# A hybrid RG-LRU / GLA / PEER step on one core: weight slabs laid out on the host, 8 KB per partition and slab instead of 1 KB

## The reference

```python
for l in range(DEPTH):                       # DEPTH = 2
    mod_p = ada_mod(c_ctx[None], ada_w[l], ada_b[l])      # silu(cond) @ ada_w[l], 1024 x 6144
    mod_s = ada_mod(c, ada_w[l], ada_b[l])
    hp = pre_mod(xp, norm1_g[l], mod_p[0], mod_p[1])      # rmsnorm * (1 + scale) + shift
    ...
    # l even: proj = xm @ rg_w_in (1024 x 2048); conv; block-diagonal gates (rg_wa, rg_wi);
    #         linear scans in both directions; (gelu(gate) * h) @ rg_w_out (1024 x 1024)
    # l odd:  proj = xm @ gla_w_in (1024 x 3104: q, k, v, g and 32 columns z);
    #         chunked GLA in both directions; (silu(g) * norm(o)) @ gla_w_out (1024 x 1024)
    xp = xp + mod_p[2] * op
    xp = xp + mod_p[5] * peer(pre_mod(xp, norm2_g[l], mod_p[3], mod_p[4]), *pp)

def peer(xm, wq, k1, k2, u_tab, v_tab):      # 8 heads, 16 experts of 16384 per token and head
    q = xt @ wq                              # wq 1024 x 2048, 256 columns per head
    # scores against two sets of 128 keys, top 16 of each, top 16 of the sums, softmax -> gate
    act = gelu(einsum(x, u_tab[eid]))        # gathered rows of 4 KB
    out = einsum(gate * act, v_tab[eid])     # gathered rows of 4 KB
```

## Time and profile before

| what | value |
|---|---|
| median of 3 runs | 3019.55 us (3008.57 to 3032.76) |
| span of the profiled execution | 2689.4 us |
| the profiled execution's own time | not given with the page; the median is 330 us above the span |
| TensorE matmul busy | 2146.1 us (80%) |
| VectorE busy | 1636.2 us (61%) |
| ScalarE busy | 510.5 us (19%) |
| GpSimd busy | 1514.9 us (56%) |
| moved by DMA | 912.92 MB, mean 339 GB/s |
| q0 (gathers) | 805.40 MB, 75.9% of 16 DMA engines' span |
| q1 (SP) | 101.20 MB, 11.6% |
| q10 (ScalarE) | 5.39 MB, 0.7% |

### The profile page before, as it was taken

How to read it: one execution, slowest core, us unless ns; L and a number is a source line. 1 busy time by engine, 2 the same in 40 slices (tenths; PEclk the granted TensorE clock), 3 DMA queues, 4 the chain that set the end, 5 groups by cost and what they waited for, 6 DMA issues and landing times.

```text
span 2689.4 us, 25633 instructions
## 1 busy us (share of the span) xinstructions
PE 2146.1 (80%) x6324; PEld 1057.5 (39%) x6324; DVE 1636.2 (61%) x3913; ACT 510.5 (19%) x1291; POOL 1514.9 (56%) x1543
## 2 busy tenths in 40 slices
PE   6999695967878786776899996777777777777777
PEld 2555442423333333332447653333333333333333
DVE  3224568677676675767433436767667675767665
ACT  2160211111111111121242122111111211111112
POOL 0000377777777777677500006777777676767774
PEclk9999797989888898887989997888888888888889
DMA  9984499999999999999723118999999999999996
GB/s 294 313 259 163 169 407 403 407 410 407 410 400 410 407 410 396 410 408 409 303 68 95 59 35 321 407 381 398 399 405 389 383 408 396 393 393 382 410 409 255
DMA packets 326341, 912.92 MB, mean 339 GB/s; under 512 B 31952, under 2 KB 128464, under 8 KB 325744
## 3 DMA queue, kind: packets, MB, share of 16 engines
q0 software_dynamic: 221184, 805.40, 75.9%
q1 hardware_dynamic: 97840, 101.20, 11.6%
q10 hardware_dynamic: 7232, 5.39, 0.7%
HBM read 909.26 MB, written 2.63 MB: 339 GB/s over the span
## 4 chain that ended last, share of the span: by engine, by line
PE 38%; issue 21%; DMA 17%; DVE 12%; POOL 9%; ACT 1%; ACTq 1%; POOLq 1%; DVEq 0%
PE psum L727 16%; DMA arena<-in_peer_u,idx 16%; PE psum L670 9%; POOL arena L326 6%; POOL arena L332 4%; PE psum L708 3%; PE psum L635 3%; PE psum L849 2%; DVE arena L1086 1%; PE psum L657 1%; PE psum L927 1%; PE psum L788 1%; DVE i12u L1034 1%; DVE small L1052 1%; ACTq L362 1%
## 5 line engine op out<-in xcount | busy, mean ns | idle before, releaser
L727 PE MATMUL psum<-arena,diag 128*128 128x512 f32 x3072 | 1409.8, 621 | 476.4 <-ACT diag L467 476.4
L326 POOL DMA_INDIRECT arena<-in_peer_u,idx x768 | 762.1, 992 | 908.1 <-issue 520.8
L1086 DVE SCALAR_TENSOR_TENSOR arena<-arena,xtok 128x1024 f32<-128x1024 f32 x768 | 940.6, 1225 | 539.4 <-DMA arena<-in_peer_u,idx 510.4
L727 PEld LDWEIGHTS psum<-arena,diag 128*128 128x128 f32 x3072 | 609.1, 200 | 1266.7 <-issue 817.7
L332 POOL DMA_INDIRECT arena<-in_peer_v,idx x768 | 748.8, 975 | 234.2 <-issue 228.7
L467 ACT ACTIVATE diag<-ident,wts 128x128 f32<-128x128 f32 x768 | 270.2, 394 | 534.2 <-PE psum L727 499.3
L670 PE MATMUL psum<-arena,slab 128*128 128x384 f32 x672 | 226.1, 494 | 6.9 <-DMA slab<-in_rg_w_out 4.7
L670 PEld LDWEIGHTS psum<-arena,slab 128*128 128x128 f32 x672 | 127.6, 192 | 99.8 <-issue 11.5
L708 PE MATMUL psum<-area 128*128 128x384 f32 (+1 forms) x512 | 160.9, 473 | 0.0
L461 ACT ACTIVATE tanh<-inner 128x16 f32<-128x16 f32 (+2 forms) x52 | 11.1, 213 | 676.6 <-DVE inner L1093 676.5
L708 PEld LDWEIGHTS psum<-area 128*128 128x128 f32 x512 | 97.2, 190 | 63.9 <-issue 6.7
(11 more groups left out here) (205 smaller groups left out, 1389.7 us busy)
## 6 DMA issues: line engine op xcount, KB each, us to landing
slab<-in_ada_w SPq DMA_DIRECT2D x33, 1024.0 KB, 8.3
area<-in_peer_wq SPq DMA_DIRECT2D x16, 1024.0 KB, 16.5
arena<-in_peer_u,idx POOLq DMA_INDIRECT x768, 7.8
arena<-in_peer_v,idx POOLq DMA_INDIRECT x768, 7.9
slab<-in_gla_w_in SPq DMA_DIRECT2D x12, 1024.0 KB, 5.4
keys<-in_ada_w SPq DMA_DIRECT2D x8, 1024.0 KB, 7.8
area<-in_ada_w SPq DMA_DIRECT2D x7, 1024.0 KB, 8.7
slab<-in_rg_w_in SPq DMA_DIRECT2D x5, 1024.0 KB, 11.5
```

The lines of the kernel that those rows point to most:

```text
L326: pool.indirect_dma_start(ubuf[j % US], None, u_rows, bass.IndirectOffsetOnAxis(ap=idx[t][:, j:j + 1], axis=0)).then_inc(u_in[j % US], 16)
L727: mm = pe.matmul(acc[t][:, half * 512:(half + 1) * 512], diag[j % DS][:, :], vbuf[j][:, half * 512:(half + 1) * 512], start=False, stop=Tr ...
L1086: dve.scalar_tensor_tensor(ubuf[j % US], ubuf[j % US], 1.0, xtok[:, t * D:(t + 1) * D], ALU.mult, ALU.mult, accum_out=dots[t][:, j:j + 1]) ...
```

## The change

The host lays out `ada_w`, `peer_wq`, `rg_w_in`, `rg_w_out`, `gla_w_in` (its first 3072 columns) and `gla_w_out` by slabs: [slab, 128, 8, 256], so that the 8 KB of a partition are one contiguous piece. The 32 columns for `wz` become an input of their own, [128, 8, 32], 1 KB per partition. In the kernel only the sources of these DMAs change. Order, buffers, waits, sizes and destinations of all instructions stay.

```diff
--- before.py
+++ after.py
@@ -101,7 +101,7 @@
 
 
 def build(nc, x_t, pos_t, vecs, ident_d, mask_d, iota_d, keys_t, ada_w, peer_wq, peer_u, peer_v, rg_w_in,
-          rg_wa, rg_wi, rg_w_out, gla_w_in, w_alpha, state_gla, gla_w_out, y_t, st_rg, st_gla):
+          rg_wa, rg_wi, rg_w_out, gla_w_in, gla_wz, w_alpha, state_gla, gla_w_out, y_t, st_rg, st_gla):
     ctx = ExitStack()
     with ctx:
         def sb(name, shape, dt=F32):
@@ -250,28 +250,25 @@
                 else:
                     sp.wait_ge(sem("g_mm"), 2 * (j - 8) + 2)
 
-            sources = {"rg_in": rg_w_in[0], "rg_out": rg_w_out[0], "gla_in": gla_w_in[0, :, 0:3 * D],
-                       "gla_out": gla_w_out[0]}
+            sources = {"rg_in": rg_w_in, "rg_out": rg_w_out, "gla_in": gla_w_in, "gla_out": gla_w_out}
 
             def stream(first, end):
 
                 for k in range(first, end):
                     name, j = SEQ[k]
-                    w = ada_w[j // 24] if name == "ada" else sources[name]
-                    n = j % 24 if name == "ada" else (j + 4) % 8 if name == "rg_in" else j
+                    w = ada_w if name == "ada" else sources[name]
+                    n = (j + 4) % 8 if name == "rg_in" else j
                     if BEFORE[k] is not None:
                         wait_used(BEFORE[k])
-                    sp.dma_start(slab[SLOT[k]][:, :, :],
-                                 w.rearrange("(c p) n -> p c n", p=P)[:, :, n * SW:(n + 1) * SW]
-                                 ).then_inc(slab_in[SLOT[k]], 16)
+                    sp.dma_start(slab[SLOT[k]][:, :, :], w[n]).then_inc(slab_in[SLOT[k]], 16)
 
             def stream_wq(layer):
 
-                src = peer_wq[layer].rearrange("(c p) n -> p c n", p=P)
-                sp.dma_start(wq_slab, src[:, :, 0:SW]).then_inc(wq_in, 16)
+                sp.dma_start(wq_slab, peer_wq[PH * layer]).then_inc(wq_in, 16)
                 with sp.Fori(1, PH) as h:
                     sp.wait_ge(sem("q_mm"), h * 2 + 2 * PH * layer)
-                    sp.dma_start(wq_slab, src[:, :, bass.ds(h * SW, SW)]).then_inc(wq_in, 16)
+                    sp.dma_start(wq_slab, peer_wq[bass.ds(h + PH * layer, 1)].rearrange("o p c n -> p (o c) n")
+                                 ).then_inc(wq_in, 16)
 
             stream(0, PLACE["gla_in", 0])
             wait_used(LAST_IN[SLABS])
@@ -353,8 +350,7 @@
                            ACT.Silu).then_inc(sem("cond_ready"), 1)
             act.dma_start(ident[:, :], ident_d).then_inc(const_in, 16)
             act.dma_start(iota16[:, :], iota_d).then_inc(const_in, 16)
-            act.dma_start(wz[:, :, :], gla_w_in[0].rearrange("(c p) n -> p c n", p=P)[:, :, 3 * D:3 * D + 2 * RANK]
-                          ).then_inc(gla_small_in, 16)
+            act.dma_start(wz[:, :, :], gla_wz).then_inc(gla_small_in, 16)
             act.wait_ge(sem("bd_zero"), 1)
             for kind, w in enumerate((rg_wa, rg_wi)):
                 for d in range(2):
@@ -1320,6 +1316,12 @@
     def to_feat(x):
         return np.ascontiguousarray(x.T.reshape(C, P, -1).transpose(1, 0, 2))
 
+    def slabs(w):
+
+        return w.reshape(-1, C, P, w.shape[-1] // SW, SW).transpose(0, 3, 2, 1, 4).reshape(-1, P, C, SW)
+
+    gla_w = a["gla_w_in"][:, :, 0:3 * D]
+    gla_wz = a["gla_w_in"][0, :, 3 * D:].reshape(C, P, 2 * RANK).transpose(1, 0, 2)
     x = np.concatenate([a["x_prompt"][0], a["x_sample"][0]], axis=0)
     vecs = np.zeros((P, V_END), f)
     vecs[:, V_COND:V_COND + 8] = feat(a["c_ctx"])
@@ -1344,10 +1346,10 @@
     arrays = {
         "x_t": to_feat(x), "pos_t": to_feat(pos), "vecs": vecs, "ident": np.eye(P, dtype=f), "mask": mask,
         "iota": np.tile(np.arange(TOPK, dtype=f), (P, 1)), "keys_t": keys,
-        "ada_w": a["ada_w"], "peer_wq": a["peer_wq"], "peer_u": a["peer_u"], "peer_v": a["peer_v"],
-        "rg_w_in": a["rg_w_in"], "rg_wa": a["rg_wa"], "rg_wi": a["rg_wi"], "rg_w_out": a["rg_w_out"],
-        "gla_w_in": a["gla_w_in"], "w_alpha": a["gla_w_alpha"], "state_gla": a["state_gla"][0, 0],
-        "gla_w_out": a["gla_w_out"],
+        "ada_w": slabs(a["ada_w"]), "peer_wq": slabs(a["peer_wq"]), "peer_u": a["peer_u"], "peer_v": a["peer_v"],
+        "rg_w_in": slabs(a["rg_w_in"]), "rg_wa": a["rg_wa"], "rg_wi": a["rg_wi"], "rg_w_out": slabs(a["rg_w_out"]),
+        "gla_w_in": slabs(gla_w), "gla_wz": gla_wz, "w_alpha": a["gla_w_alpha"], "state_gla": a["state_gla"][0, 0],
+        "gla_w_out": slabs(a["gla_w_out"]),
     }
     arrays = {k: np.ascontiguousarray(v) for k, v in arrays.items()}
     nc = bacc.Bacc("TRN2", target_bir_lowering=False, num_devices=1)
```

## The result

| kernel | median of 16 runs | range |
|---|---|---|
| before | 3032.3 us | 3008.57 to 3064.31 |
| after | 3064.85 us | 3048.25 to 3086.96 |

The ratio is 1.0101, with a 95% interval of 1.0072 to 1.013. The change makes the kernel 1% slower, 31 us of 3032, and the time lies above the range of 2996 to 3040. The profiled execution of after spans 3070.9 us and took 3072.74 us by itself. So 1.8 us lie around the span, and not 330: the profiled execution of before, with its span of 2689.4 us, was an execution that no timed one is like. The fastest of all timed runs of before in this study took 3004 us.

What follows compares the result with a forecast made beforehand. It took PEER as bound by DMA and the RG-LRU and GLA stages as bound by TensorE. Start +12, PEER -9.0 and small terms -0.5 gave +2.5 us on 3019.55: 3022 us, range 2996 to 3040.

Steps and rivals of the forecast that it cites:

- The start: First stage: ScalarE's small-row loads take turns with 8 KB packets, so L365 and TensorE's squares come later: +12 us.
- Rival (a): At the start ScalarE isn't blocked by its queued packets, squares begin 6.7 us earlier: 3003 us, 18%.
- PEER, the gain: PEER stages, taken as bound by DMA: 18 slabs each take 0.50 us less from the gathers: -9.0 us.
- Rival (c): In PEER 8 KB packets starve the gathers, up to 2.5 us more per slab, 45 us: 3067 us, 4%.
- Rival (b): Long rows buy nothing beside PEER's gathers and the start still loses 12 us: 3031.5 us, 13%.
- The base: Whole kernel: the median before the change, 3019.55 us, to which the forecast's terms were added.
- the 330 us are taken as they are: Gap between profiled span (2689.4 us) and median (3019.55): put outside the span, untouched by the change.
- Small terms: First rg_out slab before the output projection arrives sooner, -0.5 us; GLA slabs, gla_wz and simpler access patterns cost nothing.

Runs made afterwards that it cites:

- e11: The kernel before with only ada_w and the RG-LRU matrices by slabs, and the new wz: ratio 1.0048 to before.
- e2: The kernel after with the block-diagonal gate weights laid out whole by the host and loaded in one DMA instead of eight: ratio 1.0009 to before.
- e16: The kernel before with 132 extra, unused loads of peer_wq slabs in PEER's head loops, in 1 KB rows: 3155.57 us, ratio 1.0261 to before.
- e1: The kernel before, unedited, profiled and timed once more: 3065.89 us, ratio 1.0006 to before.
- e15: The kernel before with peer_wq by slabs and 132 extra, unused loads of its slabs in 8 KB rows: 3287.0 us, ratio 1.067 to before.
- e4: The kernel after with peer_wq in the old layout: ratio 1.0018 to before.
- e3: The kernel before with peer_wq alone by slabs: ratio 1.0029 to before.
- e13: The kernel before with only the GLA matrices and wz by slabs: ratio 0.999 to before.
- e17: The kernel before with ada_w and the RG-LRU matrices by slabs and the block-diagonal gate weights in one load, second timing: ratio 0.9953 to before.
- e18: e6 again without edit, which is e17 with the GLA matrices by slabs as well: ratio 1.0004 to before.
- e6: The kernel after with the block-diagonal gate weights in one load and peer_wq in the old layout: ratio 1.0034 to before.

## Why the prediction was wrong

**The start: right.** ScalarE's last issue ends at 37.48 us, L361 begins at 37.52 (37.3 forecast) and the squares at 45.15 (45.2). Nothing makes up for it: the first gathers of the five kernels with this start come at 315.4 to 316.1 us, those of the ten with the old one at 300.9 to 305.0, medians 12.6 us apart (12 forecast), and e11 costs 15 us (its interval is 5 to 25). That 133 packets were queued at the end and not 143 is worth 10 x 0.020 = 0.2 us.

**Rival (a): ruled out.** It needed a ScalarE that is not held. Only with the eight loads made one does that come about (L355 at 8.20 us in e2).

**PEER, the gain: this is the step that failed.** It took the stage as bound by DMA, so that half a microsecond saved per slab was half a microsecond less of time: -9.0 us. The half microsecond itself is there. Alone in flight, from 60 to 67 us of after, 8 KB rows move at 430 GB/s, where 1 KB rows had 349:

```profile
DMA packets 415, 3.01 MB, mean 430 GB/s; under 512 B 48, under 2 KB 48, under 8 KB 48
```

But time of the DMA engines is not what is short in PEER: e16 moves 138 MB more, 353 us at its own 392 GB/s, and takes some 80 us longer. In ordinary executions the gathers, the dot products, the `tanh` and the indices wait for one another (e1), at 349 and not at 407 GB/s. With long rows the runs show a cost where the forecast has a gain: 0.9 us per slab in e15 against e16, and with the start's share taken off, 18 us of the change's 31.

How a slab can cost more in long rows is seen where both queues have rows waiting. They take equal turns there as well. SP's slabs and the gathers in after, from 1173.5 to 1176 us:

```profile
q1 hardware_dynamic: 87, 0.71, 67.2%
q0 software_dynamic: 88, 0.35, 33.9%
```

and in e1, from 1158 to 1170 us:

```profile
q0 software_dynamic: 1017, 3.71, 79.4%
q1 hardware_dynamic: 1014, 1.02, 24.4%
```

Beside 8 KB rows the gathers get 0.35 MB / 2.5 us = 140 GB/s, beside 1 KB rows 3.71 / 12 = 309. One whole slab of `peer_wq` in after, from 695.2 to 701.3 us:

```profile
q0 software_dynamic: 340, 1.26, 51.0%
q1 hardware_dynamic: 139, 1.01, 44.8%
```

and in e1, from 684.7 to 696 us:

```profile
q0 software_dynamic: 957, 3.49, 78.1%
q1 hardware_dynamic: 1006, 1.01, 25.9%
```

The slab lands in 6.1 us and not in 11.3, as the prediction had it in kind. But the gathers beside it get 1.26 MB / 6.1 us = 207 GB/s, against 3.49 / 11.3 = 309. Against the stage's 349 GB/s they fall behind by 6.1 x (349 - 207) = 0.87 MB in after and by 11.3 x (349 - 309) = 0.45 MB in e1; the difference is 1.2 us at 349 GB/s. With the rates of the equal turns, a slab takes 3.7 and 12.3 us and the same working gives 0.8 us. These are estimates that take the chain's mean rate as its need; they lie near the 0.9 us of e15 and e16.

The four slabs of `gla_in` at the end of the layer can't be sized so. In after the gathers are absent for 8 of the burst's 15 us (from 1177 to 1185 us), but GpSimd had stopped issuing at 1169.8, before the burst, and waits 11.89 us for indices; in e1 it waits 8.49 us at the same place. At the price of the others, 18 slabs at 0.8 to 1.2 us make 14 to 22 us. The change as a whole costs 31 (1.0103 in the mean of three), of which the start takes 13, which leaves 18. The forecast had -9.5 here.

The parts don't add up cleanly, though. e2 is after without the loss at the start; 18 us would be 1.006, above its interval (1.0009, up to 1.0045). e4 is after with `peer_wq` in short rows; 13 us and the four `gla_in` slabs would be some 1.005; it has 1.0018 (0.9981 to 1.0056). Each edit alone seems to take away more than its share.

**Rival (c) named the mechanism and was dismissed on the wrong row.** 8 KB packets do take the DMA engines from the gathers while a slab is in flight (equal turns, above), and the time lost is not caught up (e15 against e16); that it is the chain that fails to catch up is argued. The prediction held against it that VectorE and TensorE have 27 us of slack in a head. That slack is that of an execution of 2689 us. In ordinary ones the slack of each engine is larger still (TensorE is busy 581 of 860 us in after), and time is lost all the same. Its size was overstated: 2.5 us per slab, of which some 0.9 came, net of the 0.5 saved. That its 3067 us lie so near the 3064.85 measured is chance: it had +47 us on 3019.6, and measured are +31 on 3032.3.

**Rival (b)** (nothing bought, the start lost, +12) is ruled out by e15 and e16, where the row length matters beside gathers, and by 31 us where it has 12. The rule of the Trainium skill ("DMA: Bandwidth & Descriptors", Specifications), by which 512 B are enough for line rate, would have kept the gain out of the sum. The traces do not agree with it: alone in flight 1 KB rows move at 349 GB/s and 8 KB rows at 430. Its 3031.5 us lie nearer to the measured time than 3022 all the same, though not for its reason.

**The base.** The median of before is 3032.3 us over 16 runs and was 3019.55 over three, so 13 of the 43 us by which 3022 missed are of the base; the other 30 are the 28 of PEER (18 for -9.5) and 1 of the start, to rounding. The step "the 330 us are taken as they are" put them outside the span; 1.8 us are there. The difference lies inside PEER: from the first to the last gather the two layers take 1024 and 1037 us in the first profile and 1192 and 1224 in e1, and with them goes the regime on which the failed step rested.

**Small terms.** TensorE waits 4.3 us before the output projection, 4.5 in e1 and 4.7 in the first profile, so -0.2 to -0.4 for -0.5. (The 5.15 us of the earlier trace rows are the transfer's piece of the chain and not the wait.) Between the squares and 227 us TensorE waits for no slab, as forecast; it waits 2.4 us for ScalarE right behind the squares, as in e1.

**Still open.** (1) Why the first profiled execution was over 300 us shorter than any other. Its granted clock in PEER is higher as well (0.88 against 0.82); whether that is a cause or a consequence, no run separates. (2) How the 18 us divide, and by which wait they are lost. The heavy dose gives 0.9 us per slab, the light one 0.3 with an interval that includes 0; e3 has 9 us, from -2 to 20; e13 has -3, yet e17 and e18, which differ in the GLA matrices alone, lie 0.5% apart; e2 has `peer_wq` in long rows and 1.0009, e6 and e18 (one kernel) have it in short ones and 1.0034 and 1.0004. (3) What becomes of an early start. e17's squares begin 9.5 us before those of e1, its first gather 3.7 us before the median of the ten with the old start, and its time is 14 us less; neither the loss on the way nor the gain behind it is explained. A version of after with `bd` loaded late, behind ScalarE's first computations, was not tried.

## What to carry to other kernels

Compare the span of a profiled execution with the timed median before pricing anything by it; where they differ by 10%, a second profile is worth more than any argument. In these traces DMA queues that share engines take turns by the row (468 to 466, 87 to 88), so the row length of one queue sets how long the small rows of another wait, and how long an engine that issues them is held (25.6 us beside 1 KB rows, 37.5 beside 8 KB). Long rows moved faster alone (430 GB/s for 349) and cost time beside the gathers here. Load small scattered tables in one DMA (e2); issuing them behind the first computations of their engine is the other way, not tried here. And try the doubtful resource: adding 138 MB of transfers (e16) showed what a DMA share of 0.9 had hidden, that in its ordinary executions the stage was not bound by DMA.

## What was not expected of the hardware

The kernel before had one execution in which the gathers ran at 396 to 408 GB/s with a granted clock of 0.88, and otherwise ones like e1, with 339 to 349 GB/s and 0.82. Even there the DMA engines can do more: with 132 more slabs in 1 KB rows they moved 392 GB/s (e16), and the kernel took only 2.6% longer for 15% more bytes (138 MB beside 913). In 8 KB rows the same bytes cost 6.7%. And the number of packets that may be queued on ScalarE's queue when an issue ends was 142 and 143 in one kernel and 133 in the other.
